# A two-block fp32 transformer on one core: the first block's norms from three sums taken with the branch's chunks, and the first attention heads staged early

## The reference, cut to what matters

```python
def rmsnorm(x, g):
    y = xf * lax.rsqrt(jnp.mean(xf * xf, axis=-1, keepdims=True) + RMS_EPS)
    return y * g

h = rmsnorm(x, norm_mix_pre[l])
...                                   # w_in, pooling, convolution, dilated attention, gates
x = x + rmsnorm(merged @ w_out[l], norm_mix_post[l])
h = rmsnorm(x, norm_mem_pre[l])
mem_n = rmsnorm(mem, norm_memkv[l])
x = x + rmsnorm(memory_cross_attention(h, mem_n, ...), norm_mem_post[l])
h = rmsnorm(x, norm_ffn_pre[l])
y = (silu(causal_dwconv(ua, conv_ffn_w[l])) * ub) @ w_down[l]
x = x + rmsnorm(y, norm_ffn_post[l])
```

## Time and profile before

| | us |
|---|---|
| median of three runs | 4032.6 (4029.64 to 4035.18) |
| the profiled execution | 4029.22 |
| its span | 4027.0 |
| mean granted clock of PE | 0.965 of 2.4 GHz |

### The profile page before, as it was taken

How to read it: one execution, slowest core, us unless ns; L and a number is a source line. 1 busy time by engine, 2 the same in 40 slices (tenths; PEclk the granted TensorE clock), 3 DMA queues, 4 the chain that set the end, 5 groups by cost and what they waited for, 6 DMA issues and landing times.

```text
span 4027.0 us, 51915 instructions
## 1 busy us (share of the span) xinstructions
PE 3710.4 (92%) x18978; PEld 3038.4 (75%) x18978; DVE 2082.1 (52%) x3529; ACT 1516.5 (38%) x2325; POOL 234.2 (6%) x351
## 2 busy tenths in 40 slices
PE   7999988999899998899969889799999798989997
PEld 5788865888687886688748668688888587877885
DVE  4633456777663345677763454443333436755443
ACT  3233354332333334533244355432122325643222
POOL 0000000001000000000000153000000002410000
PEclk9999999999899999999989899999999899999998
DMA  3222322446331233144631500112222121112332
GB/s 119 94 63 77 96 89 79 141 145 203 96 97 63 73 95 100 63 146 141 195 96 63 78 9 1 42 52 63 63 63 64 40 74 31 29 42 73 94 98 69
DMA packets 114241, 334.06 MB, mean 83 GB/s; under 512 B 34479, under 2 KB 35247, under 8 KB 113455
## 3 DMA queue, kind: packets, MB, share of 16 engines
q1 hardware_dynamic: 83087, 269.06, 22.2%
q0 software_dynamic: 14400, 52.44, 4.1%
q10 hardware_dynamic: 16608, 10.61, 1.1%
HBM read 329.97 MB, written 6.97 MB: 84 GB/s over the span
## 4 chain that ended last, share of the span: by engine, by line
PE 81%; DVE 8%; ACT 5%; DVEq 2%; issue 2%; DMA 1%; POOL 1%; ACTq 0%; POOLq 0%; SPq 0%
PE PS L566 13%; PE PS L568 13%; PE PS L567 13%; PE PS L919 10%; PE PS L916 10%; PE PS L917 10%; PE PS L616 2%; PE PS L704 2%; PE PS L1018 1%; PE PS L961 1%; PE PS L713 1%; PE PS L1042 1%; PE PS L981 1%; DVE HVAL L1843 1%; ACT PB L1569 1%
## 5 line engine op out<-in xcount | busy, mean ns | idle before, releaser
L1799 DVE TENSOR_TENSOR WL<-RAW,WH 128x1024 fp32r<-128x1024 f32 x494 | 604.4, 1224 | 535.2 <-ACT WH L1242 531.5
L1242 ACT ACTIVATE WH<-RAW 128x1024 fp32r<-128x1024 f32 x494 | 521.4, 1056 | 682.5 <-PE PS L919 363.4
L566 PE MATMUL PS<-HHI,WH 128*128 128x512 f32 x1632 | 658.0, 403 | 41.7 <-DVE HLO L1836 36.4
L568 PE MATMUL PS<-HHI,WL 128*128 128x512 f32 x1632 | 644.5, 395 | 0.0
L567 PE MATMUL PS<-HLO,WH 128*128 128x512 f32 x1632 | 642.5, 394 | 0.0
L916 PE MATMUL PS<-H2HI,WH 128*128 128x512 f32 (+1 forms) x1432 | 512.6, 358 | 37.4 <-DVE H2LO L2249 34.4
L917 PE MATMUL PS<-H2LO,WH 128*128 128x512 f32 (+1 forms) x1432 | 484.7, 354 | 0.0
L919 PE MATMUL PS<-H2HI,WL 128*128 128x512 f32 (+1 forms) x1432 | 422.1, 355 | 0.0
L566 PEld LDWEIGHTS PS<-HHI,WH 128*128 128x128 f32 x1632 | 309.8, 190 | 127.9 <-issue 47.0
L568 PEld LDWEIGHTS PS<-HHI,WL 128*128 128x128 f32 x1632 | 310.4, 190 | 72.4
L567 PEld LDWEIGHTS PS<-HLO,WH 128*128 128x128 f32 x1632 | 310.9, 191 | 63.5 <-issue 0.5
(11 more groups left out here) (357 smaller groups left out, 5967.1 us busy)
## 6 DMA issues: line engine op xcount, KB each, us to landing
RAW<-in_stream SPq DMA_DIRECT2D x494, 512.0 KB, 3.5
MODW<-in_modw POOLq DMA_DIRECT2D x96, 512.0 KB, 4.4
bias_rows<-in_rpb SPq DMA_DIRECT2D x1, 4762.5 KB, 55.2
MEM<-in_mem ACTq DMA_DIRECT2D x3, 1024.0 KB, 4.8
X<-in_x SPq DMA_DIRECT2D x1, 2048.0 KB, 9.1
CROW<-in_crow POOLq DMA_DIRECT2D x4, 512.0 KB, 4.5
out<-X SPq DMA_DIRECT2D x1, 2048.0 KB, 7.1
BIAS<-bias_rows ACTq DMA_DIRECT2D x8, 224.0 KB, 4.6
```

Of the source, the lines that this page charges most:

```text
L566: nc.tensor.matmul(out, WH[:, slot, b * P:(b + 1) * P], hi, start=start, stop=False)
L568: return nc.tensor.matmul(out, WL[:, slot, b * P:(b + 1) * P], hi, start=False, stop=stop)
L1242: A(WH[:, d, :], RAW[:, s, :], ACT.Copy).then_inc(high_split, 1)
L1799: TT(WL[:, d, :], RAW[:, s, :], WH[:, d, :].bitcast(F32), ALU.subtract).then_inc(split_ready, 1)
```

## The change

Names below are those of the diff.

1. Three sums are taken while a branch's chunks come in. ACT's `branch` writes Y already multiplied by the gain g, and squares y (`SQ_Y`) and g*y (`SQ_G`). DVE's `add_moments` multiplies x by g*y and adds the three products up over the chunks in `SUMS`. With r the post-norm root, the sum of squares of the new x is (sum x^2) + 2 r (sum x g y) + r^2 (sum (g y)^2), so the pre-norm root is known before x is updated. `SUM_X` carries the sum on from norm to norm.
2. The sums over partitions are matmuls with the data as weights and one column of ones as the moving operand (`column_sums`): four per 512 tokens, result 128x4 with the tokens on partitions. The last chunk's products are added by four more each. The roots are Sqrt on 128x4 on ACT and a reciprocal on DVE. `spread` brings a root back to all partitions with four matmuls against the identity, into PSUM.
3. `residual_and_norm` makes residual and norm in one pass over the chunks; `chunk_pair` works on two units at once, the second `LAG` = 4 chunks behind the first. It waits for both units' splits at its start.
4. In the last chunk of the down projection the last split moves behind the chunk (on DVE behind `residual_and_norm`), and a modulation row moves ahead.
5. The second block's first layer takes the root of X from the first block; only the context is squared and summed.
6. The first head's Q and K of both attentions are staged during the projection (`STAGED_AT` = 13), with other homes for the tiles.
7. The relative-position rows go by 8 DMAs on ACT's queue during full attention instead of one on SP's; the identity is loaded ahead of X.

```diff
-BIAS_HEADS = 2 * HEADS + 2
+BIAS_HEADS = 2 * HEADS
+STAGED_AT = 13
+LAG = 4
...
+            def column_sums(dst, src, start, stop):
+                for c in range(4):
+                    last = nc.tensor.matmul(dst[:, c:c + 1], src[:, c * P:(c + 1) * P], ONES[:, 0:1], start=start and c == 0, stop=stop, skip_group_check=True)
+                return last
...
+            def moments(b):
+                pe.wait_ge(mom_sum, 18 * (b + 1))
+                for dst, src in zip((MOM_YY, MOM_XY, MOM_GG), SUMS):
+                    column_sums(dst, src, dst is not MOM_GG, False)
+                pe.wait_ge(taken[1], m.at("use1", 1))
+                column_sums(MOM_YY, SQ_Y[1], False, True).then_inc(mom_done, 1)
+                pe.wait_ge(mom_xy, b + 1)
+                column_sums(MOM_XY, XY[:], False, True).then_inc(mom_done, 1)
+                pe.wait_ge(mom_sq, KB * (b + 1))
+                column_sums(MOM_GG, SQ_G[1], False, True).then_inc(mom_done, 1)
+
+            def spread(n, dst, r):
+                pe.wait_ge(mom_inverse, n)
+                for c in range(4):
+                    last = nc.tensor.matmul(dst[:, c * P:(c + 1) * P], r[:, c:c + 1].to_broadcast([P, P]), IDENT[:], start=True, stop=True)
+                last.then_inc(mom_spread, 1)
...
+            def chunk_pair(hi, lo):
+                slots = [(m.n["units"] + x) % SLOTS for x in range(2)]
+                pe.wait_ge(split_ready, m.at("units", 2))
+                for slot in slots:
+                    set_in(slot)
+                for k in range(KB + LAG):
+                    if k < KB:
+                        m.add("lo")
+                        pe.wait_ge(lo_ready, m.at("lo"))
+                        last = products(bank(3 * slots[0]), slots[0], k, hi[:, k, :], lo[:, k, :], k == 0, k == KB - 1)
+                        if k == KB - 1:
+                            unit_out(last)
+                    if k >= LAG:
+                        last = products(bank(3 * slots[1]), slots[1], k - LAG, hi[:, k - LAG, :], lo[:, k - LAG, :], k == LAG, k == KB + LAG - 1)
+                unit_out(last)
...
-                statistics(T)
...
+                moments_at, spread_at = 1, 2
+                for k in range(KB):
+                    if k == moments_at:
+                        moments(3 * l)
+                    if k == spread_at:
+                        spread_both(3 * l)
                     chunk(NHI, NLO, TC)
...
-                m.add("sq", KB // 2)
-                statistics(T)
-                sum_squares(T)
+                moments(3 * l + 1)
+                spread_both(3 * l + 1)
+                chunk_pair(HHI, HLO)
...
+            def branch(b, k, src, gain, evacuated):
+                A(Y[:, k, :], src, ACT.Identity, scale=PL[:, gain + k:gain + k + 1]).then_inc(mom_y, 1)
+                if k >= 2:
+                    act.wait_ge(mom_sum, 18 * b + 3 * (k - 1))
+                sq = A(SQ_Y[k % 2], src, ACT.Square, scale=D ** -0.5)
+                if evacuated is not None:
+                    sq.then_inc(evacuated, 1)
+                act.drain()
+                A(SQ_G[k % 2], Y[:, k, :], ACT.Square, scale=D ** -0.5).then_inc(mom_sq, 1)
...
+            def add_moments(b, k):
+                xy = SUMS[1] if k == 0 else XY[:]
+                dve.wait_ge(mom_y, KB * b + k + 1)
+                if k >= 2:
+                    dve.drain()
+                multiplied = TT(xy, X[:, k, :], Y[:, k, :], ALU.mult)
+                if k == KB - 1:
+                    multiplied.then_inc(mom_xy, 1)
+                elif k:
+                    dve.wait_ge(mom_sq, KB * b + k + 1)
+                    dve.drain()
+                    TT(SUMS[0], SQ_Y[0] if k == 1 else SUMS[0], SQ_Y[k % 2], ALU.add).then_inc(mom_sum, 1)
+                    TT(SUMS[2], SQ_G[0] if k == 1 else SUMS[2], SQ_G[k % 2], ALU.add).then_inc(mom_sum, 1)
+                    TT(SUMS[1], SUMS[1], XY[:], ALU.add).then_inc(mom_sum, 1)
...
+            def inverses(b):
+                dve.wait_ge(mom_root, 2 * b + 2)
+                nc.vector.reciprocal(R_POST, ROOT_POST).then_inc(mom_inverse, 1)
+                dve.wait_ge(mom_done, 3 * b + 3)
...
+                TS(SUM_X, MOM, 0.0, None, ALU.max).then_inc(mom_pre, 1)
+                dve.wait_ge(mom_root, 2 * b + 3)
+                nc.vector.reciprocal(R_PRE, ROOT_PRE).then_inc(mom_inverse, 1)
...
+            def residual_and_norm(b, gain, between=None):
+                dve.wait_ge(mom_spread, 2 * b + 2)
+                times_root(0)
+                dve.drain()
+                to_x(0)
+                times_root(1)
+                dve.drain()
+                dve.wait_ge(mom_spread, 2 * b + 3)
+                for k in range(KB):
+                    normed(k, gain)
+                    if k + 1 < KB:
+                        to_x(k + 1)
+                    if k + 2 < KB:
+                        times_root(k + 2)
+                    normed_low(k)
+                    dve.drain()
+                    if between is not None and k + 1 < KB:
+                        between()
...
+                inverses(3 * l + 2)
+                if l + 1 < DEPTH:
+                    residual_and_norm(3 * l + 2, lambda k: PAR[:, l + 1, G_MIX + k:G_MIX + k + 1])
+                else:
+                    residual_alone(3 * l + 2)
+                    dve.wait_ge(mom_spread, 2 * DEPTH * 3 + 1)
+                    nc.vector.tensor_copy(RS[:, 0:T], SPREAD_PRE)
+                split_low()
...
-                sum_squares(TA)
+                sum_squares(TA, 0 if l else T)
...
+                    if t == STAGED_AT + 2 and l == 0:
+                        dve.wait_ge(full_kept, 2)
+                        TT(U2R[:, 0, :], U2[:, 0, :], FULL_QH[0].bitcast(F32), ALU.subtract)
+                        TT(U2R[:, 4, :], U2[:, 4, :], FULL_KH[0].bitcast(F32), ALU.subtract).then_inc(full_first, 1)
```

More of the change, by code:

```diff
@@ L649, in attention @@
                 outputs(count - 1)
-            pe.wait_ge(x_in, 16 * 4)
+            pe.wait_ge(x_in, 16 * 5)
             sum_squares(TC)
-            sum_squares(T)
-            pe.wait_ge(consts_in, 16 * 5)
-            for _ in range(DEPTH):
-                chunk(HHI, HLO, ready=True)
-                chunk(HHI, HLO)
+            first_sums()
+            spread(1, SPREAD_PRE, R_PRE)
+            pe.wait_ge(consts_in, 16 * 4)
+            for l in range(DEPTH):
+                chunk_pair(HHI, HLO)
                 with m.loop(pe, (C_V - 2) // 2, units=2, use0=1, use1=1):
@@ L836, in _ @@
                 pe.wait_ge(mem_ready, m.at("mem"))
-                for _ in range(KB):
+                moments_at, spread_at = 1, 2
[4 more added lines that the diff above has]
+                        spread_both(3 * l)
                     chunk(NHI, NLO, TC)
-                statistics(T)
-                chunk(HHI, HLO, ready=True)
-                for _ in range(HEADS - 1):
+                chunk_pair(HHI, HLO)
+                for _ in range(HEADS - 2):
                     chunk(HHI, HLO)
@@ L1444, in _ @@
                         unit_passed()
-                squares(of_y, T)
-                act.preload_act_table(ACT.Ln)
-                root(T)
-                squares(of_x, T, before=lambda k: take(KV[:, k:k + 1, :], TC))
-                act.preload_act_table(ACT.Ln)
-                root(T)
-                norm_high()
+                for k in range(KB):
+                    p = unit_wait()
+                    m.add(f"use{p}")
+                    branch(3 * l, k, bank(3 * p), G_MIXP, taken[p])
+                    split_high()
+                act.preload_act_table(ACT.Sqrt)
+                take(KV[:, 0:1, :], TC)
+                post_root(3 * l)
+                pre_root(3 * l)
+                take(KV[:, 1:2, :], TC)
+                for k in range(KB):
+                    high(HHI[:, k, :], HVAL[:, k, :])
+                    if k + 2 < KB:
+                        take(KV[:, k + 2:k + 3, :], TC)
                 for c in range(HEADS):
@@ L1838, in norm_apply, with times_root, to_x, normed @@
+            def times_root(k):
+                TT(Y[:, k, :], Y[:, k, :], SPREAD_POST, ALU.mult)
+            def to_x(k):
+                TT(X[:, k, :], X[:, k, :], Y[:, k, :], ALU.add).then_inc(x_ready, 1)
+            def normed(k, gain):
+                STT(HVAL[:, k, :], X[:, k, :], gain(k), SPREAD_PRE, ALU.mult, ALU.mult).then_inc(val_ready, 1)
+            def normed_low(k):
+                low(HLO[:, k, :], HVAL[:, k, :], HHI[:, k, :])
             def norm_apply(gain):
-                dve.drain()
+                dve.wait_ge(mom_spread, 1)
```

265 lines of the change are left out of this document (131 added, 134 removed).

## The result

| | us | ratio to before |
|---|---|---|
| kernel before, runs beside it | 4031.1 (4026.3 to 4035.2) | |
| changed kernel, 4 runs | 4069.1 (4067.3 to 4071.0) | 1.0095 [1.0081, 1.0109] |
| its profiled execution's span | 4066.2 | before 4027.0 |

What follows compares the result with a forecast made beforehand. PE, busy 92% of the span, was taken as the bound, with time to gain where it waits at norm boundaries. The terms summed to 25.4 us off 4029.2, giving 4003.8; with 3.4 for the runs' median, 4007, range 3986 to 4024.

Steps and rivals of the forecast that it cites:

- start: Start: a root swaps Ln, table load and Exp for Sqrt, reciprocal and a cold spread; gain 0.3 us, bounds -1 and 2.
- after w_out, two layers: Boundary after w_out: second query unit ends sooner than 569.4; gain 5.5 us a layer, 11.0 in all, bounds 3 and 9 each.
- w_mo and after it, two layers: After w_mo: last `HLO` at 670.8 against 666.3; loss 4.4 us each, 8.8 in all, bounds gain 1, loss 8.
- w_down of layer 0, after it: After w_down of layer 0: `chunk_pair` waits for the late second split; gain 0.5 us, or 10 without that wait.
- w_down of layer 1: Inside w_down as a whole: DVE needs 14.4 us of PE's 15.1 a chunk; 0.5 us lost, bounds 0 and 20.
- last w_down to block 2: After the last w_down: context load issued earlier, root ready at 2083.0 against 2097.3; gain 14.3 us, bounds 11 and 16.
- heads, two attentions: First maximum of each attention comes sooner: 4.3 us in full attention, 4.8 in the second; 9.1 in all, bounds 6 and 10.5.
- the 0.5 of the DMA issues: Eight DMA issues on ACT's queue at 0.34 us, where ACT has idle time; 0.5 us lost, bounds 0 and 2.7.
- A column sum at 0.22 us, `moments` 5.3: Norm boundaries: 24 column sums at 0.22 us, so `moments` takes 5.3 us at full clock, 10.6 at the low one.
- the turns: In w_mo ACT's squares and DVE's sums run in turn: 3.4 us a chunk, 3.85 with split and product between.
- (b): Rival: small matmuls at low clock throughout, turns cost more; w_mo loses 8 each, w_out gains 3 each; 4019; chance 0.20.
- (c): Rival: slower, every chunk's sums hold up the splits of w_out and w_down; 4052 at 2 us more; chance 0.05.

Runs made afterwards that it cites:

- E4: The changed kernel with the MOMS tile 64 floats wide instead of 24, which brings back the old distance's step: 4028.4 us, ratio 0.9997.
- E2: The kernel before with only an unused tile of 24 floats (96 bytes) added between MR and MOD: 4078.14 us, ratio 1.0114.
- E9: E4 run once more, unchanged, for its profile: 4027.9 us.
- E8: E7 with the column sums after w_out in six groups of four among the first key unit's products: 4005.8 us, ratio 0.9936.
- E7: Changed kernel, MOMS 48 wide, with ACT's square wait loosened and the late split put before `residual_and_norm` in layer 0's w_down: 4004.8 us, ratio 0.9946.
- E10: E7 with squares and sums in fp32r, each column sum one matmul against two columns of ones, halving the instructions of `moments`: 3984.7 us, ratio 0.9881.
- M1: TensorE alone, returning x: units of 24 128x512 matmuls with moving tiles, weights or both shifted, 27 cases; .2290 us a matmul unshifted.
- M2: TensorE alone again: further distances, 512 and 256 column pairs, column sums alone or among products; .2269 us a matmul at 112 floats.

## Why the prediction was wrong

It had every boundary but not the tile's address: no term for a shift of the activations stood in the sum. That is the first step that failed: a shift was put at nothing, without a reason. It costs +41 us (E4 against the changed kernel; +48 in the kernel before, E2) and decides the sign. The rest, 25 us forecast and none found at the old distance, is in the terms. The ends of the same splits in E4 and E9 less those of before give each stage at the old distance:

| step | forecast | E4 | E9 |
|---|---|---|---|
| start | -0.3 | -1.1 | +0.5 |
| w_out itself (two layers) | 0 | +1.6 | +1.6 |
| after w_out, two layers | -11.0 | -0.7 | +0.3 |
| w_mo and after it, two layers | +8.8 | +17.4 | +17.4 |
| w_down of layer 0, after it | 0, -0.5 | +2.4, -0.7 | +2.3, -0.7 |
| w_down of layer 1 | +0.5 | +1.0 | +3.2 |
| last w_down to block 2 | -14.3 | -13.7 | -15.2 |
| heads, two attentions | -9.1 | -11.0 | -11.6 |

(The forecast gave 0.5 lost for w_down as a whole; it is put to layer 1 here, and the 0.5 of the DMA issues has no row. What is left to the whole, +8.8 in E4 and +2.3 in E9, is mostly the start of `up` in layer 1 of block 2, +2.8 in both, which E8 has as well and E7 has not, and E4's slow units.)

- *A column sum at 0.22 us, `moments` 5.3.* This is the step that failed among the terms. Cost per instruction was right (0.10 at the full clock), but I took the full clock, after w_mo all but the start, and kept the low one as a bound. In E4 it fell within `moments` itself: 8.0 us after w_out, 10.3 after w_mo, 7.5 after w_down. It does not fall at the same place each time: the changed kernel's profile has 5.3 to 8.2 after w_out and E7's 5.3 and 6.3, with the fall behind the sums, in the key unit (4.4 us in E7's layer 0).
- *After w_out:* 2.7 us longer sums and a key unit slower by 2.1 (4.9 for 2.8) are 4.8 of the 5.2 that the forecast gain of 5.5 a layer lacks. E10 bears this out: in its layer 0, with sums of 2.6 us and a key unit of 3.0 (5.3 and 4.4 in E7), the boundary ends 4.2 us sooner than in E7. The rest of the chain was right: 3.78 us for an iteration with a split, the pair held until the seventh split.
- *After w_mo:* the turns came as forecast (7.23 us a unit, the sums of chunk 6 within 0.3 us of the forecast), and the loss has the right sign, but it is 8.7 instead of 4.4 each: `moments` takes 3.0 us more than the 7.3 I gave it, and the rest of the difference is small pieces, 0.3 of them its start. The turns that I priced were not its cause: without them (E7) it is 0.5 to 1.4 less.
- *After w_down, layer 0:* the pair's first product did come behind the late split, 1.4 us behind the last `HLO` where I had 1.2, and E7 shows the 10 us that I gave for its absence (11.7).
- *After the last w_down* came out: the context's DMA is issued 18.2 us behind the last unit (2118.07 less 2099.84), 18 forecast. *The heads* did better, 11.0 and 11.6 for 9.1, beyond the upper bound of 10.5: the first attention gave 3.6 and 4.1 (4.3 forecast), the second 7.4 and 7.5 (4.8).
- Of the rivals, (b) had the mechanism of the boundaries and too small a size: it kept a gain of 3 each after w_out. (c), the only slower one, did not happen: its signs, waits for `WL` inside w_out and w_down, make at most 1.6 us in w_out and 3.4 to 5.5 in w_down, of which some 2 in E9 are its slow units. No rival held the address.

Open: why the distance matters within 256 bytes, what the low tile's own distance does, why the change is worth 7 to 9 us at two distances and nothing at the old one, when exactly the clock falls, and why single executions have stretches of 5.60 us units.

## What to carry to other kernels

Measure the step of the most frequent matmul before and after any change of the memory layout, even a few floats; in a kernel that PE bounds, place new tiles behind the operands or pad to the old distance, and try the other distances. A stream of one-column matmuls is to be sized at both clocks even where PE has no gap, and what stands behind it too; halving its instructions gave 20 us here. Priced waits deserve an experiment: two of them, taken away by three edited lines, gave 13 us, nearly all of it from one.

## What the runs showed of the hardware

- A 128x512 fp32r matmul takes .2268 to .2351 us a step by the distance between weights and moving operands modulo 256 bytes (M1, M2), 3.7% from best to worst; both moved together, nothing changes; of two moving tiles in turn, one moved alone makes another step (.2334 with 48 floats, where both moved give .2268).
- The granted clock fell to 0.50 without an idle gap within 48 one-column instructions or just behind them (E4, E7, M2), and also with them among 256-column products (E8 in layer 0, M2). It stayed at 1.00 in E8's layer 1 and among 512-column products (M2).
- A one-column fp32 matmul costs two instructions of 0.10 us at the full clock and 0.21 at the low one; a two-column fp32r matmul one of 0.11 and 0.21 (E10). The Trainium skill (TensorE: Matmul & The Clock Gate, "Wait — 56ns, not 53.3ns?") gives a floor of 25 ns between starts for small matmuls; with 128x128 weights changed at each, these rows lie four times above it.
